# Input projection of a gated recurrence by seven block products instead of eight, with the conv, gate and scan work re-slotted around it

## What is computed

```
proj = h @ w_in                              # 512 x 1024 by 1024 x 2048
y_branch, x_branch = split(proj, 2)
gate = gelu(y_branch)                        # tanh form
xc   = causal_depthwise_conv(x_branch)       # width 4
r, i = sigmoid(xc @ ga_w + ..), sigmoid(xc @ gx_w + ..)   # 8 blocks of 128 x 128
a    = exp(-8 * r * softplus(-lam))
u    = sqrt(1 - a^2) * (i * xc)
hr_t = a_t * hr_{t-1} + u_t                  # scan over tokens
out  = (gate * hr) @ w_out
```

## Time and profile before

| | |
|---|---|
| median of 3 runs | 3449.39 us (3446.28 to 3449.89) |
| the profiled execution | 3450.99 us, of it the span 3449.4 us |
| busy, share of the span | PE 96%, DVE 58%, POOL 30%, ACT 21% |
| the recurrence's stretch | about 2013 to 2145 us of the span |
| mean granted TensorE clock | 0.99 of full |

### The profile page before, as it was taken

How to read it: one execution, slowest core, us unless ns; L and a number is a source line. 1 busy time by engine, 2 the same in 40 slices (tenths; PEclk the granted TensorE clock), 3 DMA queues, 4 the chain that set the end, 5 groups by cost and what they waited for, 6 DMA issues and landing times. The chain is left out here.

```text
span 3449.4 us, 39911 instructions
## 1 busy us (share of the span) xinstructions
PE 3327.8 (96%) x15432; PEld 2474.5 (72%) x15432; DVE 2005.4 (58%) x3518; ACT 719.7 (21%) x1548; POOL 1031.7 (30%) x800
## 2 busy tenths in 40 slices
PE   5999999999999999999999999999999998999998
PEld 4567775555555556778888854888886885688887
DVE  7666377666766443267545656654444786665543
ACT  2243231100000224131111124111111233311110
POOL 0110223333233000224444401444441550244443
PEclk9999999999999999999999999999999999999999
DMA  6332321333331121231222221222222220022222
GB/s 259 107 115 80 105 67 49 123 119 112 122 110 61 61 70 51 68 92 62 86 87 86 87 84 61 86 86 86 86 98 86 80 84 28 26 75 91 91 86 86
DMA packets 63580, 301.70 MB, mean 87 GB/s; under 512 B 7232, under 2 KB 19648, under 8 KB 37280
## 3 DMA queue, kind: packets, MB, share of 16 engines
q1 hardware_dynamic: 51872, 260.87, 22.5%
q0 software_dynamic: 6528, 18.75, 1.7%
q10 hardware_dynamic: 4992, 19.53, 1.6%
HBM read 294.27 MB, written 2.88 MB: 86 GB/s over the span
## 5 line engine op out<-in xcount | busy, mean ns | idle before, releaser
L2590 POOL TENSOR_TENSOR scratch<-ring 128x512 f32<-128x512 f32 (+1 forms) x160 | 224.2, 1401 | 1527.6 <-PE psum L694 1116.6
L694 PE MATMUL psum<-big,scratch 128*128 128x256 f32 (+1 forms) x2240 | 607.6, 427 | 4.8 <-DVE big L2025 4.8
L694 PEld LDWEIGHTS psum<-big,scratch 128*128 128x128 f32 x2240 | 426.0, 190 | 169.6 <-issue 8.2
L694 PE MATMUL psum<-H,scratch 128*128 128x256 f32 (+1 forms) x2144 | 500.7, 389 | 3.6 <-ACT cb L1352 3.6
L694 PEld LDWEIGHTS psum<-H,scratch 128*128 128x128 f32 x2144 | 405.9, 190 | 84.0 <-ACT cb L1352 8.9
L665 PE MATMUL psum<-H,ring 128*128 128x512 f32 x928 | 423.1, 607 | 13.4 <-ACT H L1434 11.5
L694 PE MATMUL psum<-big,ring 128*128 128x256 f32 (+1 forms) x1584 | 426.0, 422 | 8.7 <-issue 3.2
L694 PE MATMUL psum<-H,ring 128*128 128x256 f32 (+1 forms) x1536 | 402.9, 407 | 8.3 <-ACT H L1434 4.2
L694 PEld LDWEIGHTS psum<-big,ring 128*128 128x128 f32 x1584 | 303.0, 192 | 115.3 <-issue 5.3
L694 PEld LDWEIGHTS psum<-H,ring 128*128 128x128 f32 x1536 | 297.6, 195 | 83.4 <-issue 9.1
L665 PEld LDWEIGHTS psum<-H,ring 128*128 128x128 f32 x928 | 175.1, 194 | 221.7 <-issue 216.4
(11 more groups left out here) (361 smaller groups left out, 4133.7 us busy)
## 6 DMA issues: line engine op xcount, KB each, us to landing
ring<-in_wall SPq DMA_DIRECT2D x202, 1024.0 KB, 4.9
big<-in_wada SPq DMA_DIRECT2D x48, 512.0 KB, 3.6
big<-in_wada POOLq DMA_DIRECT2D x32, 512.0 KB, 3.8
big<-in_wada ACTq DMA_DIRECT2D x4, 2048.0 KB, 20.4
scratch<-in_rpb ACTq DMA_DIRECT2D x16, 512.0 KB, 4.5
X<-in_xin SPq DMA_DIRECT2D x4, 768.0 KB, 11.8
scratch<-negd SPq DMA_DIRECT2D x8, 384.0 KB, 8.3
big<-negd SPq DMA_DIRECT2D x8, 384.0 KB, 9.3
```

The costliest lines, as they stand in the source:

```text
L694: mm = pe.matmul(fast_bank(st, q, b), lhsT, rhs(k), start=start and k == 0, stop=k == kt - 1, skip_group_check=True)
L2590: pool.tensor_tensor(s1, a21, a22, ALU.add).then_inc(combo_own, 1)
```

## The change

The input projection becomes a stage `LRU` of the fast kind, with 8 slots, the three rotating banks of `HEADS`, and its pieces in `wx`. Its two branch tiles per slot (2x and 2x+1) land directly in `XB` (slots 0 to 3) or `GT` (4 to 7). The conv's first tap and the gelu square now read the SBUF copy (`lru_tokens`). `T2` moves from `scratch` to `cb`, and POOL mixes the eight slots without waiting for `lru_input`. The gates' matmuls go behind product 6 (odd tiles) and product 4 (even tiles) of slots 0 to 4. On DVE the tile work is cut in two parts per slot (`branch_tiles`), part 0 between products 2 and 3, part 1 behind product 7, with a table for the scans. The scalings of the residual go: two into slot 2, six behind the first three slots of `YA`. Three semaphores of the rotary tables become one.

The core of the diff, with renumberings of stages and semaphores left out:

```diff
-        T2 = [S_[:, b * 512:(b + 1) * 512] for b in range(4)]
+        T2 = [cb[:, b * 512:(b + 1) * 512] for b in range(4)]
...
+        def lru_branch(t):
+            return XB[:, t, CONV - 1:CONV - 1 + SEQ] if t < DT else GT[:, t - DT, :]
...
         def fast_bank(st, q, i):
-            if st is HEADS:
-                return bank(((0, 1, 2), (2, 0, 1), (1, 2, 0))[(q - st.q0) % 3][i], st.width())
+            if st in (HEADS, LRU):
+                turn = (q - st.q0 + (st is LRU)) % 3
+                return bank(((0, 1, 2), (2, 0, 1), (1, 2, 0))[turn][i], st.width())
...
-            for s in range(8):
-                project(xq, normed=32 if s == 0 else None,
-                        after=lambda f, s=s: lru_gates(2 * s + f - 1) if 1 <= 2 * s + f <= DT else None)
-            for p in range(2):
-                pe.wait_ge(acc_free[p], w.unit // 2)
+            def between_branches(x, i):
+
+                if i == 6 and 1 <= x <= 4:
+                    lru_gates(2 * x - 1)
+                if i == 4 and x < 4:
+                    lru_gates(2 * x)
+
+            fast_stage(LRU, between=between_branches)
...
+                    if kind == "lru":
+                        if x in (4, 5):
+                            lru_roots(x - 4)
+                        if 1 <= x <= 4:
+                            lru_tile(2 * x - 1)
+                        if x >= 5:
+                            gelu_tanh(2 * x - 9)
+                        lru_tokens(q, 2 * x)
...
                     if x + 1 < len(slots):
                         copy(q + 1, 1)
+                    if kind == "lru":
+                        act.wait_ge(prod[4], q + 1)
+                        act.activation(lru_branch(2 * s + 1)[:, 0:256], fast_bank(st, q, 1), ACT.Copy).then_inc(c21_done, 1)
+                        act.wait_ge(c21_done, q + 1)
+                        lru_tokens(q, 2 * x + 1)
+                        if x < 4:
+                            lru_tile(2 * x)
+                        else:
+                            gelu_tanh(2 * x - 8)
...
+            def lru_tokens(q, t):
+
+                act.wait_ge(c22_done if t % 2 else c12_done, q + 1)
+                if t < DT:
+                    act.activation(XC[:, t, :], lru_branch(t), ACT.Identity, bias=v("conv_b", t), scale=v("conv_w", 24 + t))\
+                       .then_inc(lru_copied, 1)
                 else:
-                    i = u - DT
+                    i = t - DT
                     if i >= 2:
                         act.wait_ge(gelu_done, i - 1)
-                    act.activation(GT[:, i, :], src, ACT.Copy)
...
+                def to_branches(q, x):
+
+                    a, b = lru_branch(2 * x), lru_branch(2 * x + 1)
+                    took(2, q, c11_done, a[:, 0:256], 1)
+                    branch_tiles(x, 0)
+                    took(3, q, c12_done, a[:, 256:512], 6)
+                    took(7, q, c22_done, b[:, 256:512], 5)
+                    branch_tiles(x, 1)
...
+                        if st is YA and s < 3:
+                            final_scale(2 * s + 2)
+                            final_scale(2 * s + 3)
+                            own.wait()
...
             norm(4, None)
+            mix_hidden_input(LRU)
+            own(dve.tensor_copy(rstd_s[:], bank(5)))
...
+            SCANS = [{5: (1,), 6: (4,), 7: (6,)}, {4: (0,), 5: (2, 3), 6: (5,), 7: (7,)}]
+
+            def branch_tiles(x, part):
+
+                t = 2 * x + part - 1
+                if 0 <= t < DT:
+                    conv(t)
+                if 0 <= t - 1 < DT:
+                    lru_input(t - 1)
+                if x == 2:
+                    final_scale(part)
+                i = t - DT
+                if i >= 0:
+                    gelu_cube(i)
+                for c in SCANS[part].get(x, ()):
+                    lru_scan(c)
+                if i >= 1:
+                    gated(i - 1)
+
+            fast_stage(LRU, branch_tiles)
+            gelu_cube(DT - 1)
+            gated(DT - 2)
             gated(DT - 1)
...
-            pool.wait_ge(lru_v, DT)
+            mix_weights(LRU)
             mix_weights(YA)
```

More of the change, by code:

```diff
@@ L102, in slots @@
             return [("heads", 0, s) for s in range(12)]
+        if self.kind == "lru":
+            return [("lru", 0, s) for s in range(8)]
         if self.kind == "relu":
@@ L118 @@
 MLP = [Stage("relu", True, 18, 4, 1, 0, 8, 40, 0, 2), Stage("relu", False, 68, 40, 3, 16, 24, 40, 1, 4)]
-YA, SW0 = Stage("y", False, 108, 72, 4, 0, 0, -1, 2, 5), Stage("gated", False, 112, 76, 5, 32, 40, -1, 2, 6)
-HEADS = Stage("heads", False, 152, 110, 6, 0, 0, -1, 2, 8)
-YB, SW1 = Stage("y", False, 164, 122, 7, 0, 0, -1, 2, 7), Stage("gated", False, 168, 126, 8, 43, 64, -1, 3, 8)
-STAGES = [Y[0], MLP[0], Y[1], MLP[1], YA, SW0, HEADS, YB, SW1]
-N_FAST = 160
+LRU = Stage("lru", False, 100, 72, 4, 0, 32, -1, 2, 8)
+YA, SW0 = Stage("y", False, 108, 80, 5, 0, 0, -1, 2, 5), Stage("gated", False, 112, 84, 6, 32, 40, -1, 2, 6)
+HEADS = Stage("heads", False, 152, 118, 7, 0, 0, -1, 2, 8)
+YB, SW1 = Stage("y", False, 164, 130, 8, 0, 0, -1, 2, 7), Stage("gated", False, 168, 134, 9, 43, 64, -1, 3, 8)
+STAGES = [Y[0], MLP[0], Y[1], MLP[1], LRU, YA, SW0, HEADS, YB, SW1]
+N_FAST = 168
 FAST = {st.slot0 + x: st.q0 + x for st in STAGES for x in range(len(st.slots()))}
@@ L749, in fast_stage @@
                     pe.wait_ge(combos_ready, q + 1)
-                    if rotated:
+                    if rotated or st is YA and x == 0:
                         pe.wait_ge(c21_done, q)
@@ L1685, in gelu_tanh @@
                 act.activation(GB[i % 2], GB[i % 2], ACT.Tanh, scale=GELU_C).then_inc(gelu_sig, 1)
-            for u in range(2 * DT):
-                half(u % 2)
-                src = acc(w.unit)
-                if u < DT:
-                    act.activation(XB[:, u, CONV - 1:CONV - 1 + SEQ], src, ACT.Copy)
-                    act.activation(XC[:, u, :], src, ACT.Identity, bias=v("conv_b", u), scale=v("conv_w", 24 + u))\
-                       .then_inc(acc_free[w.unit % 2], 1)
+            def lru_tokens(q, t):
[3 more added lines that the diff above has]
+                       .then_inc(lru_copied, 1)
                 else:
-                    i = u - DT
+                    i = t - DT
                     if i >= 2:
                         act.wait_ge(gelu_done, i - 1)
-                    act.activation(GT[:, i, :], src, ACT.Copy)
-                    act.activation(GB[i % 2], src, ACT.Square, scale=0.044715 ** 0.5).then_inc(acc_free[w.unit % 2], 1)
-                w.unit += 1
-                w.slot += u % 2
-                if 2 <= u < 2 + DT:
-                    lru_tile(u - 2)
-                if u in (7, 11):
-                    lru_roots(u // 8)
-                if u > DT:
-                    gelu_tanh(u - DT - 1)
+                    act.activation(GB[i % 2], GT[:, i, :], ACT.Square, scale=0.044715 ** 0.5).then_inc(lru_copied, 1)
+            fast_stage(LRU)
             gelu_tanh(DT - 1)
@@ L2467, in gated, with final_scale @@
                 dve.scalar_tensor_tensor(GT[:, i, :], LA[:, i, :], 0.25, GT[:, i, :], ALU.mult, ALU.mult).then_inc(hr_ready, 1)
-            for u in range(2 * DT):
-                if u < DT:
-                    conv(u)
-                else:
-                    gelu_cube(u - DT)
-                if 2 <= u < 2 + DT:
-                    lru_input(u - 2)
-                if u >= DT:
-                    lru_scan(u - DT)
-                if u > DT:
-                    gated(u - DT - 1)
-                if 1 <= u <= DT:
-                    x = X[:, u - 1, CTX:TOK]
-                    own(dve.scalar_tensor_tensor(x, x, v("final_g", u - 1), rstd_s[:], ALU.mult, ALU.mult))
+            def final_scale(k):
+                x = X[:, k, CTX:TOK]
+                own(dve.scalar_tensor_tensor(x, x, v("final_g", k), rstd_s[:], ALU.mult, ALU.mult))
+            SCANS = [{5: (1,), 6: (4,), 7: (6,)}, {4: (0,), 5: (2, 3), 6: (5,), 7: (7,)}]
[17 more added lines that the diff above has]
+            gated(DT - 2)
             gated(DT - 1)
-            skip(8, 16)
+            dve.wait_ge(prod[4], w.fast)
             mix_input(YA, lambda h, j: dve.wait_ge(hr_ready, 4 * h + j + 1))
```

34 lines of the change are left out of this document (16 added, 18 removed).

## The result

The changed kernel takes 3458.55 us (median of 8 runs, 3452.94 to 3460.59), the kernel before on the same chip 3447.89 (8 runs, 3446.28 to 3449.89): a ratio of 1.0030, 95% interval 1.0021 to 1.0039, so **10.7 us slower**. The forecast was 3455.3, range 3438 to 3463. By the prediction's own limit of 0.2% this is "slower", to which it gave 0.33, and not "the same", its likeliest word at 0.43.

The account below looks back on a forecast made before the run. PE was taken as the bound (busy 96%). Its 13 us spared went into 8.8 of gate stalls, 5.6 inside slots 5 to 7 and a longer tail: +5.9 us, 3455.3 against the median, range 3438 to 3463.

Parts of the forecast that it names:

- The start and the spared work: Projection on PE: product 5 of slot 0 starts 5.95 us after norm 4's scaling; seven products per slot spare 13.0 us.
- POOL's adds in DVE's way: Projection: each POOL mixing add costs DVE's SBUF steps 0.99 us; additions out of PSUM are not stretched.
- The gates of even tiles: Slots 0 to 3: PE waits 2.2 us for each even tile's conv, four stalls, 8.8 us.
- From slot 4 on: Slots 4 to 7: DVE is the bound; PE waits 5.6 us in slots 5 to 7, then a longer tail before YA.
- What costs nothing: YA's six scalings, slot 0's mixing, ACT's copies, SP's loads and the roots: free, bound 0 to +2 us.
- DVE also bounds YA: Rival: late DVE's sums and scalings delay YA, up to 4.5 us more, 3459.8; chance 0.15 for 3457 to 3466.
- DVE keeps the port: Rival: DVE's chained steps aren't held by POOL, gate stalls vanish, 3437.8 us; wholly or in part, chance 0.35.

Follow-up runs that it names:

- the late sums cut: Changed kernel with POOL's additions for the projection's last two slots and YA's first two cut to 4 columns in 128: 3448.88 us, ratio 1.0002.
- The throw-away matmuls: Changed kernel plus eight unused 256-column matmuls on PE ahead of YA's product 2: 3456.98 us, ratio 1.0030 to the kernel before.
- the later gates: Changed kernel with the even tiles' gates moved behind product 2 of the next slot: 3452.36 us, ratio 1.0010 to the kernel before.

## Why the prediction was right, and what it left out

All times from the start of the scaling.

- **The start and the spared work.** Right: product 5 of slot 0 came 5.94 us in (2015.08), predicted 5.95, and products take 1.73 us.
- **POOL's adds in DVE's way**, 0.99 us each and not stretching additions out of PSUM: right. The conv of tile 2, 2.33 us alone, took 4.76 (2040.36 to 2045.12), predicted 4.9. The price was read from firmer ground than I said: the earlier trace rows are not the only such passage before, since `gelu_cube` and a scan's first step at 2132.53 and 2133.69 take 1.24 and 1.75 us beside POOL's next four additions. The rule of the Trainium skill (SBUF — State Buffer, Who interferes with whom), by which each would cost a whole 1.26, would have made the slots 18.5 us long, and they are 17.7; its exclusion holds here in kind, at the smaller price.
- **The gates of even tiles.** Four stalls, right. The pitch from gate to gate is 17.68 us (2027.50 to 2045.18), predicted 17.7. The row's wait of 1.92 is less than the 2.2 predicted, but the slot loses the 2.2: part of it doesn't show as idle time. Odd tiles' gates don't wait. In the run with POOL's additions cut all four stalls are gone, so it is these that make DVE late for PE.
- **From slot 4 on.** Predicted waits 0.3 + 1.4, 2.3 and 1.6, measured 1.44, 1.83 and 0.42 + 0.57, in the places named, slot 6's at ACT's copy included. Slots 4 to 7 took 53.7 us (some 2084.1 to 2137.83), predicted 54. The last `gated` ended at 137.9, predicted 137.1, and from the end of the projection to product 5 it was 10.2 us, predicted 10.0. DVE's steps in this part are stretched by 12.3 us together, predicted 12.3. But that is not what the additions cost: with the late sums cut the stage gets 3.6 and 4.2 us back up to product 5, 7.8 in all, because DVE then waits for others instead (2.2 us for ACT in slot 5, and for PE in slots 6 and 7). DVE was the bound only while POOL held it.
- **What costs nothing.** Right for the scalings in `YA`: 45.73 us in both kernels. That also ends the rival *DVE also bounds YA* for the changed kernel. With POOL's two mixings pushed into `YA`'s slot 0 PE does wait for DVE there, 2.43 us at once; POOL's additions fall on slot 0's own additions then and not on the scalings, so the condition as I had named it was not tried.
- **DVE keeps the port**: refuted by the steps of 1.64 us.
- **The term left at zero: TensorE's clock.** The forecast says nothing of it. Product 5 of `YA` was forecast 137.6 us after the scaling and came at 138.9, and product 3 should then have followed in 3.46 us and took 5.49. Each stall was priced at its own length alone. In slot 2 the granted clock fell to the lower level (1.2 GHz; 0.50 from 2047.2 to 2049.2) behind the wait of 1.92 us, and the next gates came 19.39 us later in place of 17.7: 1.7 us. Behind the tail's waits it fell again: 5.49 - 3.46 = 2.0 us. Together 3.7 us. The stage's 9.3 exceed the forecast 5.9 by 3.4, so the other terms together were too high by 0.3. The throw-away matmuls (products 5 and 6 back at 3.46 us) and the later gates (no dip in slot 2) each show one half. So part of the agreement up to product 5, 138.9 for 137.6, is luck: without the 1.7 us of slot 2 it would have been 137.2.

So the forecast erred by 3.2 us on the median, inside its range, and by 4.8 on the difference of medians (10.7 against 5.9). Of that, 3.4 lie in the stage; the other 1.4 lie outside it and stay open, as said of the 2.4 us above. With the clock's 3.7 us the forecast would have said 3459, and "slower" as the likeliest.

## What to carry to other kernels

An engine that is moved into the same stretch is not free because it was idle: each of POOL's 128 x 512 additions cost DVE 1 us, more than the 0.69 us in which DVE makes the addition itself. Delaying POOL helps where DVE has slack behind the place that is spared (6.5 us in slots 0 to 3) and not where it has none (nothing clear at the tail). What helped as well was a consumer that asks later (6.2 us for moving the even tiles' gates), or giving the additions to the engine that is the bound (3.8 us). Taking away a wait of the late engine gains nothing if another engine's work was passing in it. And a stall of some 2 us on PE should be priced with a possible fall of the clock behind it, here 1.7 to 2 us in the changed kernel.
